# One level of Strassen's method in the upward product of a feed-forward layer, with weight sums on GpSimd, and the embedding product moved

## The reference

```python
x = x + concat([y_mla, y_diff]) @ w_out                      # out-projection
x = x + conv_ffn(rms_norm(x, ffn_norm_g), w_gate, w_up, conv_w, conv_b, w_down)
gate = sigmoid(rms_norm(x, ple_norm_g) @ w_ple_gate)
x = x + gate * (p @ w_ple_proj)                              # p: 1024 x 256

def conv_ffn(h, w_gate, w_up, conv_w, conv_b, w_down):       # w_gate, w_up: 1024 x 2816
    g = h @ w_gate
    conv = conv_b + sum over j of shifted(g, j) * conv_w[j]  # 3 taps along the tokens
    return (silu(conv) * (h @ w_up)) @ w_down
```

## Time and profile before

| what | value |
|---|---|
| runs | 2783.04, 2778.46, 2778.63 us |
| median | 2778.63 us |
| span of the profiled execution | 2782.6 us |
| mean granted TensorE clock | 0.968 |
| busy share of the span: PE, DVE, ACT, POOL | 94%, 45%, 34%, 13% |
| upward product, first to last matmul group | 1922.95 to 2409.71 us |
| embedding product up to the downward product's steady stretch | 2409.71 to 2437.05 us |
| downward product, steady stretch | 2437.05 to 2675.57 us |

### The profile page before, as it was taken

One profiled execution on the slowest core, in us unless ns is written; L12 is line 12 of the kernel. 1 busy time (PEld: TensorE's weight loads), 2 busy tenths in 40 slices (PEclk: granted clock), 3 DMA queues, 4 the chain that ended last, 5 costly groups with the idle time before them and its releaser, 6 DMA issues. The chain is left out here.

```text
span 2782.6 us, 36583 instructions
## 1 busy us (share of the span) xinstructions
PE 2615.7 (94%) x14702; PEld 2245.0 (81%) x14702; DVE 1263.3 (45%) x1770; ACT 938.4 (34%) x1549; POOL 352.8 (13%) x450
## 2 busy tenths in 40 slices
PE   8969999998799998999997989889999999999999
PEld 6849999997588886888886877767888888778877
DVE  6523444442466764543136858454233222323452
ACT  4223322221456652123115767532212111222331
POOL 1002232220332320001012223010000000000000
PEclk9979999999799998999998989989999999999999
DMA  4222121112333215443323211163222222355532
GB/s 144 86 75 82 53 77 49 53 43 64 103 117 92 74 56 185 148 137 101 122 97 102 56 41 39 35 215 92 68 69 76 71 81 68 112 180 171 189 102 80
DMA packets 215503, 264.71 MB, mean 95 GB/s; under 512 B 46852, under 2 KB 147844, under 8 KB 215336
## 3 DMA queue, kind: packets, MB, share of 16 engines
q1 hardware_dynamic: 215336, 262.38, 29.6%
HBM read 185.11 MB, written 77.22 MB: 94 GB/s over the span
## 5 line engine op out<-in xcount | busy, mean ns | idle before, releaser
L3801 PE MATMUL ffn_up_acc<-mixed_hi,ffn_ring_hi 128*128 128x512 f32 x704 | 274.9, 390 | 2.5 <-DVE mixed_lo L2922 2.5
L3801 PE MATMUL ffn_up_acc<-mixed_hi,ffn_ring_lo 128*128 128x512 f32 x704 | 274.6, 390 | 0.0
L3801 PE MATMUL ffn_up_acc<-mixed_lo,ffn_ring_hi 128*128 128x512 f32 x704 | 274.5, 390 | 0.0
L1379 PE MATMUL delta_acc<-delta_w_hi,xn_hi 128*128 128x256 f32 x640 | 192.0, 300 | 2.9 <-DVE delta_w_lo L1333 2.9
L1381 PE MATMUL delta_acc<-delta_w_hi,xn_lo 128*128 128x256 f32 x640 | 181.5, 284 | 0.0
L1380 PE MATMUL delta_acc<-delta_w_lo,xn_hi 128*128 128x256 f32 x640 | 181.4, 283 | 0.0
L3801 PEld LDWEIGHTS ffn_up_acc<-mixed_hi,ffn_ring_hi 128*128 128x128 f32 x704 | 132.6, 188 | 30.2 <-issue 2.9
L3801 PEld LDWEIGHTS ffn_up_acc<-mixed_lo,ffn_ring_hi 128*128 128x128 f32 x704 | 132.6, 188 | 27.5
L3801 PEld LDWEIGHTS ffn_up_acc<-mixed_hi,ffn_ring_lo 128*128 128x128 f32 x704 | 132.5, 188 | 27.5
L4060 DVE TENSOR_TENSOR ffn_feed_lo<-ffn_feed_raw,ffn_feed_hi 128x1536 fp32r<-128x1536 f32 x44 | 77.4, 1759 | 148.1 <-ACT ffn_feed_hi L4052 148.0
L3771 DVE TENSOR_SCALAR ffn_conv<-ffn_padded,ffn_taps 128x1024 f32<-128x1024 f32 x22 | 16.6, 753 | 276.3 <-ACT ffn_padded L3752 276.3
(11 more groups left out here) (444 smaller groups left out, 6449.7 us busy)
## 6 DMA issues: line engine op xcount, KB each, us to landing
ffn_feed_raw<-in_w_down SPq DMA_DIRECT2D x44, 512.0 KB, 3.9
ffn_ring_raw<-in_w_gate SPq DMA_DIRECT2D x11, 1024.0 KB, 5.3
ffn_ring_raw<-in_w_up SPq DMA_DIRECT2D x11, 1024.0 KB, 5.8
scratch_act_t<-ffn_silu SPq DMA_DIRECT2D x22, 512.0 KB, 2.7
ffn_feed_raw<-scratch_act_t SPq DMA_DIRECT2D x44, 256.0 KB, 3.0
delta_w_raw<-in_w_in SPq DMA_DIRECT2D x20, 512.0 KB, 4.0
scratch_projected<-delta_out SPq DMA_DIRECT2D x80, 128.0 KB, 1.7
stick_g_raw<-in_w_in SPq DMA_DIRECT2D x16, 512.0 KB, 4.6
```

Of the source, the lines that this page charges most:

```text
L1379: nc.tensor.matmul(acc, self.hi[:, k, tok], w_hi, start=(k == 0), stop=False, skip_group_check=True)
L3801: last = nc.tensor.matmul(self.acc[s][:, br, cols], weight[:, k, ch], part[:, k, cols], start=(k == 0 and first), stop=(k == 7 and weight ...
```

## The change

**Upward product.** The weight matrix of one branch and one pair of feature tiles (256 features by 1024 rows) is cut into quarters a11, a12, a21, a22 of 128 features by 512 rows; the tokens into b11, b21 (first 512 tokens, upper and lower 512 rows) and b12, b22 (last 512 tokens). One such branch and pair is a *unit* u; there are 22 (gate units are even, up units odd). A unit's four quarters of output come from seven products instead of eight, in Winograd's form:

- token sums T1 = b12 - b11, T2 = b22 - T1, T3 = T2 - b11, T4 = b21 - T2, the same for all units;
- weight sums S1 = a21 + a22, S2 = S1 - a11, S3 = a11 - a21, S4 = a12 - S2, for each unit;
- products (u,1) = a11 b11, (u,2) = a12 b21, (u,3) = S4 b22, (u,4) = a22 T4, (u,5) = S1 T1, (u,6) = S2 T2, (u,7) = S3 T3.

Each product has 4 slices and three passes: 12 matmuls (L4168 of the new kernel). `CombineTurn` takes the place of `NormTurn`; for the token tiles 4 to 7 it forms T1 and T2 on VectorE and T3 and T4 on GpSimd (four 128 x 512 instructions a tile), and splits each of them. The weight sums are four GpSimd instructions a unit, into the `xn` buffers, of which there is one set. Weights are split in pieces of 128 x 512, seven a unit, in 8 slots, 7 products ahead (`LEAD`). The outputs are combined on VectorE: U2 = (u,1) kept by ScalarE + (u,6), U4 = U2 + (u,5), quarters c22 = U4 + (u,7), c12 = U4 + (u,3), c21 = U2 + (u,4), and c11 = (u,1) + (u,2) in PSUM.

**Embedding product.** Its 96 matmuls, 16 transposes, three loads and 16 stores move into the out-projection's second half; it uses the ring's buffers and the `acc` and `turn` slots there.

**Tail.** `Feed` has new places and starts five steps before the upward product's end; `GateWeights` works in eight pieces of 512 KB, two to a step, with one raw buffer for pieces 0 to 4 and 6 and another for 5 and 7.

```diff
+class CombineTurn:
+    def vector(self, dve):
...
+                o.turn.wait_filled(dve, key)
+                nc.vector.tensor_tensor(t1, tile[:, 0:4], o.hi[:, 0:4, before].bitcast(F32), ALU.subtract).then_inc(self.t1_begun, 1)
+                nc.vector.tensor_tensor(t1, t1, o.lo[:, 0:4, before].bitcast(F32), ALU.subtract).then_inc(self.formed[0], 1)
+                nc.vector.tensor_tensor(t2, tile[:, 4:8], t1, ALU.subtract).then_inc(self.formed[1], 1)
+                o.turn.free(nc.vector.tensor_tensor(o.lo[:, 4:8, tile_of(m)], tile[:, 4:8],
+                                                    o.hi[:, 4:8, tile_of(m)].bitcast(F32), ALU.subtract), key)
+                self.keep_lo(dve, m, (0, 1))
+                if m in (5, 6):
+                    self.keep_lo(dve, m - 1, (2, 3))
...
+    def gpsimd(self, pool):
...
+                pool.wait_ge(self.formed[1], done)
+                pool.wait_ge(self.split_lo[0], done)
+                pooled.tensor_tensor(t3, t2, o.hi[:, 0:4, before].bitcast(F32), ALU.subtract).then_inc(self.t3_begun, 1)
+                pool.wait_ge(self.t3_begun, done)
+                pooled.tensor_tensor(t3, t3, o.lo[:, 0:4, before].bitcast(F32), ALU.subtract).then_inc(self.formed[2], 1)
+                pool.wait_ge(self.split_lo[1], done)
+                pooled.tensor_tensor(t4, o.hi[:, 4:8, before].bitcast(F32), t2, ALU.subtract).then_inc(self.t4_begun, 1)
+                pool.wait_ge(self.t4_begun, done)
+                pooled.tensor_tensor(t4, t4, o.lo[:, 4:8, before].bitcast(F32), ALU.add).then_inc(self.formed[3], 1)
 class FfnUp:
+    TAPS, PAIR, LEAD, SLOTS, EARLY = 3, 2, 7, 8, 1
+    AHEAD = {0: [1, 2, 3], 1: [], 2: [4, 5, 6], 3: [7, 8], 4: [9, 10], 5: [11, 12]}
+        self.order = [(0, 1), (0, 2), (1, 1), (1, 2), (0, 3), (0, 6), (0, 7), (0, 5), (1, 6), (0, 4), (1, 7), (1, 5), (1, 3)]
+        for u in range(2, self.units):
+            self.order += [(u, 1), (u, 6), (u - 1, 4), (u, 2), (u, 7), (u, 5), (u, 3)]
+        self.order.append((self.units - 1, 4))
...
+        def load(u):
+            if u >= 2:
+                sp.wait_ge(self.lo_done, self.at[(u - 2, 4)] + 1)
...
+        def first_sums(u, i):
+            a11, a21, a22 = (self.source(u, n) for n in ("a11", "a21", "a22"))
+            pool.wait_ge(self.lo_done, i)
+            pool.wait_ge(self.loaded[u % 2], 16 * (u // 2 + 1))
...
+        for step in range(1, self.total):
+            for i in self.produced(step):
+                u, product = self.order[i]
+                if product == (3 if u == 0 else 6):
+                    first_sums(u, i)
+                    second_sums(u)
+            yield
...
+    def scalar(self, act):
+        for step in range(self.total):
+            for i in self.produced(step):
+                split_hi(i)
+            u, product = self.order[step]
+            if product == 1:
+                self.wait_product(act, u, 1)
+                nc.scalar.activation(self.u2[u % 2], self.bank(u, 1), ACT.Copy).then_inc(self.p1_kept, 1)
...
+    def vector(self, dve):
+        for step in range(self.total):
+            for i in self.produced(step):
+                u, product = self.order[i]
+                if product == (3 if u == 0 else 6):
+                    dve.wait_ge(self.second_sums, 2 * u + 2)
+                split_lo(i)
+            u, product = self.order[step]
+            if product == 6:
+                nc.vector.tensor_tensor(self.u2[u % 2], self.u2[u % 2], self.bank(u, 6), ALU.add).then_inc(self.u2_done, 1)
...
+        if product == 2:
+            pe.wait_ge(self.p1_kept, u + 1)
+        elif product == 5:
+            pe.wait_ge(self.u2_done, u + 1)
+        elif product == 4:
+            pe.wait_ge(self.c22, u + 1)
...
     for m in range(TT):
         plan += [out]
+        plan += [emb] * 3 * (m == 0)
         plan += [turn] * (m >= 2) + [scale]
-        plan += [ring] * (m in (2, 4))
...
+        plan += [emb] * 4 * (1 <= m <= 4)
+        plan += [up] * (m == 2)
+    plan += [up, up, turn, up, turn, up, turn, up, turn]
...
 class GateWeights:
+        for i in range(8):
+            act.wait_ge(self.loaded[self.buffer(i)], 16 * (len(self.before(i)) + 1))
...
+            self.nc.scalar.activation(self.part(i, 0), self.raw[self.buffer(i)][:], ACT.Copy).then_inc(self.hi_done, 1)
+            if i % 2:
+                yield
```

More of the change, by code:

```diff
@@ new lines, in split, with bank @@
+    def split(self, i):
+        if i < self.EARLY:
+            parts = [t[:] for t in self.early]
+        else:
+            s = (i - self.EARLY) % self.SLOTS
+            parts = [t[1][:, s // 4, s % 4 * HALF:(s % 4 + 1) * HALF] for t in (self.ring.hi, self.ring.lo)]
+        return [part.rearrange("p (k n) -> p k n", k=4) for part in parts]
+    def bank(self, u, product):
+        i = {1: 0, 2: 0, 5: 1, 6: 1, 4: 2, 7: 2, 3: 3}[product]
+        return self.acc[u % 2][:, i // 2, i % 2 * HALF:(i % 2 + 1) * HALF]
@@ new lines, in produced, with wait_product, wait_used, wait_stored @@
+    def produced(self, step):
+        return self.AHEAD[step] if step in self.AHEAD else [i for i in [step + self.LEAD] if i < self.total]
+    def wait_product(self, eng, u, product):
+        eng.wait_ge(self.used, self.at[(u, product)] + 1)
+    def wait_used(self, eng, count):
+        eng.wait_ge(self.used, count)
+    def wait_stored(self, eng, f):
+        eng.wait_ge(self.stored[f % 2], 16 * (f // 2 + 1))
+    def sync(self, sp):
+        def load(u):
+            if u >= 2:
+                sp.wait_ge(self.lo_done, self.at[(u - 2, 4)] + 1)
+            pair = u // 2
+            sp.dma_start(self.ring.raw[u % 2][:].rearrange("p (k n) -> p k n", n=2 * P),
+                         self.weights[u % 2][:, pair * 2 * P:(pair + 1) * 2 * P].rearrange("(k p) n -> p k n", p=P)
+                         ).then_inc(self.loaded[u % 2], 16)
+        def store(f):
+            sp.wait_ge(self.multiplied, f + 1)
+            sp.dma_start(self.out[f * P:(f + 1) * P, :], self.smooth[f % 2][:]).then_inc(self.stored[f % 2], 16)
+        self.x.embedding.wait_turned(sp)
+        load(0)
+        sp.wait_ge(self.x.embedding.w_lo_done, 1)
+        load(1)
+        yield
+        sp.wait_ge(self.o.scaled, 1)
+        sp.wait_ge(self.o.left_stored, 16 * TT)
@@ L3716, in sync @@
                 sp.dma_start(self.taps_sb[:, :, tap], src.rearrange("(i p) -> p i", p=P)).then_inc(self.taps_in, 16)
-        for f, half, br in self.walk():
-            if f and half == 0 and br == 1:
-                self.store(sp, f - 1)
+        yield
+        for step in range(self.total):
+            for i in self.produced(step - 1) if step else []:
+                u, product = self.order[i]
+                if product == 4 and u + 2 < self.units:
+                    load(u + 2)
+            if step >= 2:
+                u, product = self.order[step - 2]
+                if u % 2 and product in (3, 4):
+                    store(u - 1 + (product == 4))
@@ new lines, in tensor @@
+    def tensor(self, pe):
+        nc, ready = self.nc, set()
+        yield
+        yield
+        for i, (u, product) in enumerate(self.order):
+            name = self.PRODUCTS[product][1]
+            if name not in ready:
+                self.x.wait_operand(pe, name)
+                ready.add(name)
+            pe.wait_ge(self.lo_done, i + 1)
+            self.wait_bank(pe, u, product)
+            (w_hi, w_lo), (x_hi, x_lo) = self.split(i), self.x.operand(name)
+            for k in range(4):
+                for weight, x, first in ((w_hi, x_hi, True), (w_hi, x_lo, False), (w_lo, x_hi, False)):
+                    last = nc.tensor.matmul(self.bank(u, product), weight[:, k], x[:, k],
+                                            start=(k == 0 and first and product not in (2, 4)), stop=(k == 3 and weight is w_lo),
+                                            skip_group_check=True)
+            last.then_inc(self.used, 1)
+            yield
@@ L4120, in tensor @@
                 if first and i == 0:
-                    self.embedding.release(pe, j)
+                    self.up.wait_outputs(pe, j)
                 elif first:
```

586 lines of the change are left out of this document (407 added, 179 removed).

## The result

| kernel | median of all runs shown | ratio to before, 95% interval |
|---|---|---|
| before | 2779.83 us (15 runs) | 1 |
| changed | 2784.46 us (15 runs) | 1.0019 (1.0012 to 1.0026) |

A forecast was written before the change was run, and what follows sets the result against it. TensorE's work was taken as the bound; -60.1 - 7.5 + 1 + 49.9 + 0 + 3.6 + 5 = -8.1 us gave a forecast median of 2771 us, own range 2765 to 2777, wider range 2749 to 2796.

The forecast's parts named there:

- Matmuls removed: Upward product: 1848 matmuls instead of 2112, 264 fewer at 0.2276 us each, -60.1 us.
- Waste removed and the embedding product: Lo wait, embedding waste and downward slow start go, -7.5 us; embedding work in the out-projection may bring late loads, +1.
- The start: Upward product's start: TensorE idles in three stalls (18.9, 18.2, 7.3 us), plus slow starts and small waits, +49.9 us.
- first stall: Upward product's start: TensorE idles 18.9 us before (0,1), behind token sums, inverse roots, scaling and the lo split.
- slow starts: Upward product's start: matmuls come slowly behind idle stretches, 1.6 us for each of three, 4.8 in all.
- The steady part: Upward product: VectorE's two-unit loop of 36.8 us fits within TensorE's 38.24, 1.4 us to spare, so 0 us.
- Downward product and tail: Gate weight loads delay the feed in the downward product, +3.6 us, and work in the tail, +5 us.
- Two steps of gate pieces: Downward product: two pieces share a raw buffer, 12.7 us against 10.9 for 24-matmul steps, +3.6 us for two.
- The tail: Last gate pieces' loads, issued within their steps, give about 2.5 us more in each of two steps, +5 us.
- C: Rival: no change, losses some 8 us larger by an unseen wait, 2773 to 2784 us; chance beyond forecast's range 0.13.
- A: Rival: VectorE and GpSimd pace the upward product, steady part +14.5 and start +8.6, about 2794 us; chance 0.24.
- B: Rival: cheaper start without overlap losses or slow starts, tail loads early, about 2753 us; chance 0.2, including 0.05 at 2731.

The follow-up runs named there:

- e8: Changed kernel plus e1, e2, e3, with e5 and e6 together and (0,1) split right behind token tile 5's scaling: 2741.89 us, 0.9864 of before.
- e5: Changed kernel plus e1, e2, e3, with all weight sums formed by VectorE instead of GpSimd: 2751.24 us, 0.9898 of before.
- e6: Changed kernel plus e1, e2, e3, with T4 formed by VectorE while T3 stays on GpSimd: 2756.49 us, 0.992 of before.
- e7: Changed kernel plus e1, e2, e3, with S3 formed twice, five GpSimd sums a unit instead of four: 2775.79 us, 0.9988 of before.
- e1: Changed kernel without the surplus feed step at the end of the upward product's plan: 2774.9 us, 0.9994 of before.
- e2: Changed kernel with a third raw buffer for gate weight pieces 1 and 3, loaded a step ahead: 2775.98 us, 0.9994 of before.
- e3: Changed kernel with gate weight pieces 5 and 7 loaded a step earlier, by one more gates step: 2773.86 us, 0.9985 of before.

## Why the prediction was wrong

The two traces say where the miss lies. From the out-projection's first matmul to the downward product's first (in the kernel before: 2437.05 less the 1.37 us of the six matmuls ahead of it) it is 612.7 us before and 594.0 after: -18.7 us, where -15.8 was forecast. From there to the end it is 346.9 and 369.7: +22.8 us, where +7.7 was forecast (-0.9, +3.6 and +5).

*Matmuls removed, -60.1.* Right to 0.3 us. The price of 0.2276 us was an average over a stretch that begins with a slow start. A pair of units takes 38.1 us, 0.2267 a matmul, and so did the kernel before (21.76 us for a feature tile of 96, from one convolution to the next, 2018.26 to 2040.02): 264 x 0.2267 = 59.8.

*Waste removed and the embedding product, -7.5 + 1.* On the safe side. Ahead of the downward product -18.7 is -59.8, +49.9 for the start (below), and -8.8 for the waste, where -2.5, -4.1 and +1 were charged. The +1 did not come: TensorE is full in the out-projection, and the first stall begins at the first upward product's turn. The other 2.2 us are about what the average price hid, 2112 x 0.0009 = 1.9.

*The start, +49.9.* Right. From the end of token tile 5's transposes (1959.71 less 18.66) to the downward product (2411.63) it is 470.6 us, less 418.9 for the 1848 matmuls at 0.2267 and 1.8 for two sets of transposes: 49.9. That it agrees to the digit is luck: the waits are 42.3 us instead of 44.4, the rest, slow starts above all, 7.6 instead of 5.5. The orders were read rightly: with the split for (0,1) further ahead the first stall is gone (e8), and e5 shows the price of GpSimd's weight sums. The price of moving T4 (e6) was mis-sized.

*The steady part, 0.* Right, and e7 shows the margin (about 1.2 us, 1.4 forecast).

*"Downward product and tail", +3.6 and +5.* **This step failed.** It missed one hole and mis-sized the others:

- `Feed` starts earlier and leads by one more step. The prediction has no term for that: it put the lead at nothing and gave no reason. I never asked what the additions to the residual stand behind in VectorE's order then. e1 shows what it is worth: 7 us (4.6 of wait, the rest slow start). At the start I followed each engine's order by hand; here I did not.
- Two steps of gate pieces: 5.0 us of waits instead of 3.6, since the load took 4.54 us instead of 3.9, and 1.7 us of slow start behind each, which I had charged at the start alone. e2: 7 us (8.7 in the traces) instead of 3.6.
- The tail: 6.0 us of waits more than before instead of 5, and slow starts. The 2.5 us a step of the forecast came out of no sum. e3: 9.5 us (8.5 in the traces).

Together 23.5 us by e1 to e3, where 8.6 were forecast. These 14.9 us more, less the 2.9 us that the stages ahead came out better, turn -8.1 into +3.9, against +4.1 in the traces. Of the rivals, C came nearest (a wait that I did not see), at 0.13; A and B did not happen.

## What to carry to other kernels

Where engines work strictly in a written order, a stage that is moved one step ahead has to be followed past every instruction that now stands behind it, on each engine, and at each change of phase. The places far behind the change, where no matmul was removed, cost 23.5 us, more than a third of the 60 us that the removed matmuls save. A hole in TensorE's work can have a second price, the slow matmuls behind it. It was 1.7 us behind a wait of 2.5 us and 2.7 us behind one of 17.3 us (24 matmuls in 8.14 us instead of 5.46), while e7's 18 waits of 0.7 us or less left the granted clock at 1.00. Strassen's seven products give their 12.5% in the steady part (168 matmuls in 38.1 us instead of 192 in 43.5), but the token sums and the first weight sums form a serial chain ahead of it, and on that chain sums belong on the faster engine.

## What the runs showed of the hardware

The earlier trace rows had a VectorE that kept its pace beside GpSimd, and the forecast charged GpSimd alone. At this kernel's start both lose. In the changed kernel's VectorE timeline beside GpSimd's sums of 1950.26 to 1955.19:

```profile
1950.03 0.69 DVE L3719 TENSOR_TENSOR ffn_ring_lo<-ffn_x_right,ffn_ring_hi 128x512 fp32r<-128x512 f32 x1
1950.63 1.76 DVE L3719 TENSOR_TENSOR ffn_ring_lo<-ffn_x_left,ffn_ring_hi 128x512 fp32r<-128x512 f32 x1
1952.31 1.75 DVE L3719 TENSOR_TENSOR ffn_t_lo<-ffn_x_right,ffn_t_hi 128x512 fp32r<-128x512 f32 x1
1957.44 0.75 DVE L2886 SCALAR_TENSOR_TENSOR ffn_xn<-ffn_x_left,ffn_inverse,ffn_gain_row 128x512 f32<-128x512 f32 x1 [3.38 <-POOL ffn_inverse L2852]
```

Two splits took 1.76 and 1.75 us instead of 0.69, while GpSimd's three sums took 1.58 to 1.71 instead of 1.26, 1.1 us more in all, where 1.4 was charged. VectorE's 2.1 us cost nothing here, since it then waits 3.38 us for the inverse root. The Trainium skill (GPSIMD Engine Reference, section 1) says that GpSimd shares its SBUF interfaces with VectorE and contends with VectorE's instructions that have two SBUF inputs; the trace agrees, and shows that VectorE pays as well.

In these rows the one that starts first keeps its pace. The split at 1950.03 began 0.23 us ahead of GpSimd's sum and took its 0.69 us in spite of 0.46 us of overlap, and in the earlier trace rows VectorE also began first. The two slow splits began while a sum was running, and ended 0.55 and 0.56 us behind that sum's end (1952.39 against 1951.84, 1954.06 against 1953.50), as if they had waited for it. No run tried the order by itself.
